# RWKV-7 features: no GpSimd products, the decay read one token over, both directions of a block together, the key norm in token layout; the q/k root of the DeltaNet projection moved up

## The reference, cut to what matters

```
w_log = -softplus(-(w0 + tanh(lw) @ w2)) - 0.5;  decay = exp(-exp(w_log))
a     = sigmoid(a0 + la @ a2);  gate = sigmoid(lg) @ g2
kk    = l2_normalize(heads(k * k_k))
k_dir = k * (1.0 + (a - 1.0) * k_a)
bonus = sum(r * k_dir[d] * u[d], channels of a head) * v, summed over d
```

## Time and profile before

| | |
|---|---|
| median of 3 runs | 4905.58 us (4900.68 to 4907.02) |
| the profiled execution | 4901.45 us, its span 4899.8 us |
| busy share of the span | PE 90%, PEld 80%, DVE 41%, ACT 28%, POOL 11% |
| mean granted TensorE clock | 0.939 |

### The profile page before, as it was taken

The page is one execution under the profiler, slowest core; times in us unless marked ns, Lnnn a source line. Parts: engine busy times, 40 slices in busy tenths (PEclk is TensorE's granted clock), DMA queues, the critical chain, the costliest instruction groups (busy, mean ns, idle before and its releaser), DMA issues. The chain is left out here.

```text
span 4899.8 us, 101076 instructions
## 1 busy us (share of the span) xinstructions
PE 4409.8 (90%) x43461; PEld 3932.3 (80%) x43461; DVE 1991.6 (41%) x2817; ACT 1366.0 (28%) x1958; POOL 532.2 (11%) x690
## 2 busy tenths in 40 slices
PE   6999989898948996999998999988998849996998
PEld 5998977887827995889897999977887629984887
DVE  3222254454475445322223222353444484446334
ACT  3211133232242222321113211243222242223322
POOL 1000000332032110000100000001321051100000
PEclk8999999999959998999999999999999859998999
DMA  5233231000200002233423222121000100012332
GB/s 199 79 111 109 71 112 39 14 1 4 60 7 3 4 4 78 78 124 95 154 77 112 66 62 60 59 62 35 1 0 24 47 1 4 4 42 75 97 94 69
DMA packets 344215, 286.50 MB, mean 58 GB/s; under 512 B 9086, under 2 KB 316772, under 8 KB 343396
## 3 DMA queue, kind: packets, MB, share of 16 engines
q1 hardware_dynamic: 326628, 218.92, 15.0%
q0 software_dynamic: 17280, 62.92, 3.7%
HBM read 270.27 MB, written 11.53 MB: 58 GB/s over the span
## 5 line engine op out<-in xcount | busy, mean ns | idle before, releaser
L646 PE MATMUL PS<-x_hi,w_hi 128*128 128x384 f32 (+1 forms) x2464 | 678.1, 344 | 17.6 <-DVE x_lo L550 16.1
L646 PE MATMUL PS<-x_lo,w_hi 128*128 128x384 f32 (+1 forms) x2464 | 676.3, 344 | 0.0
L646 PE MATMUL PS<-x_hi,w_lo 128*128 128x384 f32 (+1 forms) x2464 | 676.2, 343 | 0.0
L646 PEld LDWEIGHTS PS<-x_hi,w_hi 128*128 128x128 f32 x2464 | 450.3, 189 | 38.7 <-issue 24.4
L646 PEld LDWEIGHTS PS<-x_lo,w_hi 128*128 128x128 f32 x2464 | 450.2, 189 | 13.9
L646 PEld LDWEIGHTS PS<-x_hi,w_lo 128*128 128x128 f32 x2464 | 449.7, 189 | 13.7
L779 DVE TENSOR_TENSOR silu_buf<-silu_buf,PS 128x768 f32<-128x768 f32 (+1 forms) x88 | 78.1, 887 | 786.2 <-ACT silu_buf L712 786.2
L1896 PE MATMUL PS<-arena 64*64 64x64 f32 (+1 forms) x9216 | 356.9, 229 | 12.1 <-POOL arena L1879 5.6
L622 DVE TENSOR_TENSOR w_lo<-raw_w,w_hi 128x2048 fp32r<-128x2048 f32 x136 | 311.7, 2292 | 133.2 <-ACT w_hi L617 133.2
L690 PE MATMUL PS<-hidden_hi,w_hi 128*128 128x256 f32 (+1 forms) x1232 | 346.7, 351 | 19.3 <-DVE hidden_lo L784 19.3
L617 ACT ACTIVATE w_hi<-raw_w 128x2048 fp32r<-128x2048 f32 x136 | 259.5, 1908 | 338.5 <-PE PS L690 331.4
(11 more groups left out here) (341 smaller groups left out, 7803.5 us busy)
## 6 DMA issues: line engine op xcount, KB each, us to landing
raw_w<-in_ffn_w_dram SPq DMA_DIRECT2D x240, 512.0 KB, 4.4
arena<-in_ada_w_dram POOLq DMA_DIRECT2D x120, 512.0 KB, 6.1
arena<-in_w_in_dram SPq DMA_DIRECT2D x64, 512.0 KB, 3.9
arena<-in_ada_w_dram SPq DMA_DIRECT2D x6, 2048.0 KB, 14.6
raw_w<-in_ffn_w_dram SPq DMA_DIRECT2D x32, 384.0 KB, 3.5
arena<-in_w_out_dram SPq DMA_DIRECT2D x16, 512.0 KB, 4.2
h_save<-arena SPq DMA_DIRECT2D x16, 384.0 KB, 2.3
arena<-h_save SPq DMA_DIRECT2D x2, 3072.0 KB, 9.9
```

Of the source, the lines that this page charges most:

```text
L646: mm = pe.matmul(PS[:, 4 * b + 2 * g + s, 0:half], w[wo][:, k, g, :], x_split[xo][:, k, a + s * half:a + (s + 1) * half], start=(k == 0 an ...
```

## The change

- GpSimd has no work in the feature stage; its three products are made by DVE (`keys`).
- The decay up to the token before is no longer computed: KKP takes exp of minus `G` one token over within each chunk of 64 (pieces of 63), and the first token of a chunk is a copy of kk.
- The step from a to the key factor is ACT's Identity with scale and bias; the bonus is formed as (key0 u0 + key1 u1) r, the first product on ACT.
- A round is one block with both directions: gates of both, scans of both, exps of both in place of their arguments, products of both. ACT thus loads its tables once per round for Sigmoid and once for Exp.
- The first block's gates, scans and products come before the key norm. The norm's root is taken of 8 rows from one PSUM tile, turned into token layout (`pe_head_turn`), inverted as 48 columns, widened by ACT copies and spread by matmuls with the identity.
- In the DeltaNet projection the q/k root is taken at the end of place 10, between the Silus of places 9 and 10 (with a table load for each way), in place of after the last Silu.

The diff, cut to its core (of the features only the new lines; the old are printed above):

```diff
-        def pe_head_turn(pe):
+        def pe_head_turn(pe, rows=head_rows):
 
             for t in range(T // P):
-                mm = pe.transpose(PS[:, 6, 8 * t:8 * t + 8], head_rows[:, t * P:(t + 1) * P], ident[0:8, 0:8])
+                mm = pe.transpose(PS[:, 6, 8 * t:8 * t + 8], rows[:, t * P:(t + 1) * P], ident[0:8, 0:8])
...
-        HEAD_STEPS = 2 * NB + 2
+        HEAD_STEPS = 2 * NB + 3
...
                     finish(place - 1)
                     if place - 1 < 2 * NB:
                         square(place - 1)
+                if place == 2 * NB + 2:
+                    act.wait_ge(qk_summed, layer * HEAD_STEPS + 2 * NB)
+                    nc.scalar.activation(head_rows, RSTD[0:8, :], ACT.Sqrt, bias=eps[0:8, 0:1]).then_inc(qk_rooted, 1)
             finish(3 * NB - 1)
-            act.wait_ge(qk_summed, layer * HEAD_STEPS + 2 * NB)
-            nc.scalar.activation(head_rows, RSTD[0:8, :], ACT.Sqrt, bias=eps[0:8, 0:1]).then_inc(qk_rooted, 1)
 
             def split_place(place):
                 split(place // 2, place % 2)
 
             split_place(GATES + 2)
             act.wait_ge(proj_summed, 2 + layer * PT + GATES + 1)
+            act.wait_ge(conv_used, 2 + 3 * NB * (layer + 1))
...
-        E1, E2 = region(44544 + 3 * T, T), region(44544 + 4 * T, T)
+        fsq = region(46848, 2, T)
+        fsq_rows = fsq[0:8, 0, :]
+        KK_PLACE = [RSTD, PS[:, 4:6, :].rearrange("p b c -> p (b c)")[:, CTX:]]
+        KK_WIDE = [fsq[:, i, :].rearrange("p (t h c) -> p t h c", t=T // P, h=2) for i in range(2)]
+        K1 = lambda layer: 3 * NB * layer + NB
+        FE, FX = 16, 7
...
             sc = nc.scalar
             sc.activation(lora_w, lora_w, ACT.Tanh)
             sc.activation(lora_g, lora_g, ACT.Sigmoid).then_inc(lora_acted, 1)
...
             act.wait_ge(h_saved, 16 * KT * (layer + 1))
...
+            def gates(j, d):
+                J = NB * layer + j
+                act.wait_ge(lora_summed, 2 * J + d + 1)
+                if j > 0:
+                    act.wait_ge(fe_dve, FE * (J - 1) + (13 if d == 0 else 16))
                 for s, (a, w) in enumerate(SEGS):
...
+                    sc.activation(SG2[d][:, a:a + w], PS[:, 4 * d + s, 0:w], ACT.Sigmoid,
                                   bias=prm[:, layer, 1, B_W0 + d * NB + j:B_W0 + d * NB + j + 1])
...
+                    ins = sc.activation(AA2[d][:, a:a + w], PS[:, 4 * d + 2 + s, 0:w], ACT.Sigmoid,
                                         bias=prm[:, layer, 1, B_A0 + d * NB + j:B_A0 + d * NB + j + 1])
                 ins.then_inc(gates_ready, 1)
...
+                act.wait_ge(gates_ready, 2 * J + d + 1)
+                sc.activation(KD2[d], AA2[d], ACT.Identity, scale=prm[:, layer, 1, B_KA + j:B_KA + j + 1],
+                              bias=drv[:, 15 + j:16 + j]).then_inc(fe_exp, 1)
+            def decays(j, d):
+                J = NB * layer + j
+                act.wait_ge(fe_dve, FE * J + d + 1)
+                sc.activation(SG2[d], G2[d], ACT.Exp, scale=-DECAY_SCALE)
+                last = G2[d][:, RW_C - 1::RW_C] if d == 0 else G2[d][:, 0::RW_C]
                 pc = PC[:, d, j, :] if d == 0 else PC[:, d, j, ::-1]
                 sc.activation(pc, last, ACT.Exp, scale=-DECAY_SCALE).then_inc(fe_exp, 1)
...
+                act.wait_ge(fe_exp, FX * J + 3 + 2 * d)
+                sc.activation(G2[d], G2[d], ACT.Exp, scale=DECAY_SCALE).then_inc(fe_exp, 1)
+            for j in range(NB):
+                J = NB * layer + j
+                for d in range(2):
+                    gates(j, d)
+                if j == 0:
+                    for i in range(NB):
+                        act.wait_ge(kk_step, (1 + 2 * NB) * layer + i + 1)
+                        if i >= 2:
+                            act.wait_ge(kk_summed, K0(layer) + i - 1)
+                        sc.activation(fsq[:, i % 2, :], KK[:, i, :], ACT.Square).then_inc(kk_squared, 1)
+                for d in range(2):
+                    decays(j, d)
+                act.wait_ge(fe_dve, FE * J + 3)
+                sc.activation(BON[:, j, :], KD2[0], ACT.Copy, scale=prm[:, layer, 1, B_U + j:B_U + j + 1]).then_inc(fe_exp, 1)
+                if j == 0:
+                    act.wait_ge(kk_summed, K0(layer) + NB)
+                    sc.activation(fsq_rows, RSTD[0:8, :], ACT.Sqrt, bias=eps[0:8, 0:1]).then_inc(kk_rooted, 1)
+                    act.wait_ge(kk_step, (1 + 2 * NB) * layer + NB + 1)
+                    for i in range(NB):
+                        if i >= 2:
+                            act.wait_ge(kk_spread, K0(layer) + i - 1)
+                        sc.activation(KK_WIDE[i % 2], bc(tok_heads[:, :, 2 * i:2 * i + 2], 3, [P, T // P, 2, P // 2]),
+                                      ACT.Copy).then_inc(kk_squared, 1)
         def pe_feat(pe, layer):
...
             pe.wait_ge(lora_landed, 80 * (layer + 1))
             pe.wait_ge(lora_acted, layer + 1)
...
+            def lora(j, d):
+                if j > 0:
+                    pe.wait_ge(gates_ready, 2 * (NB * layer + j - 1) + d + 1)
                 rows = slice(64 * d, 64 * d + 64)
                 for o, (wt, src) in enumerate(((w2w, lora_w), (a2w, lora_a))):
                     for s, (a, w) in enumerate(SEGS):
...
+                        mm = pe.matmul(PS[:, 4 * d + 2 * o + s, 0:w], wt[rows, j * P:(j + 1) * P], src[rows, a:a + w],
                                        start=True, stop=True)
                 mm.then_inc(lora_summed, 1)
+            def spread(j):
+                pe.wait_ge(kk_squared, K1(layer) + NB + j + 1)
+                if j >= 2:
+                    pe.wait_ge(kk_step, (1 + 2 * NB) * layer + NB + j)
+                for t in range(T // P):
+                    mm = pe.matmul(KK_PLACE[j % 2][:, t * P:(t + 1) * P], fsq[:, j % 2, t * P:(t + 1) * P], ident[:, :],
+                                   start=True, stop=True)
+                mm.then_inc(kk_spread, 1)
+            lora(0, 0)
+            lora(0, 1)
+            pe.wait_ge(gates_ready, 2 * NB * layer + 2)
             for j in range(NB):
...
+                pe.wait_ge(kk_squared, K1(layer) + j + 1)
+                for a, w in SEGS:
+                    mm = pe.matmul(RSTD[0:8, a:a + w], to_pair_rows(j), fsq[:, j % 2, a:a + w], start=(j == 0), stop=(j == NB - 1))
+                mm.then_inc(kk_summed, 1)
+            lora(1, 0)
+            pe.wait_ge(kk_rooted, 2 * layer + 2)
+            pe_head_turn(pe, fsq_rows).then_inc(qk_summed, 1)
+            for j in range(NB):
+                spread(j)
+            pe.wait_ge(kk_step, (1 + 2 * NB) * (layer + 1))
+            lora(1, 1)
+            for j in range(2, NB):
+                for d in range(2):
+                    lora(j, d)
+            for j in range(NB):
+                pe.wait_ge(fe_dve, FE * (NB * layer + j + 1))
                 if j == 0:
                     pe.wait_ge(gates_ready, 2 * NB * (layer + 1))
                 for s, (a, w) in enumerate(SEGS):
...
         def dve_feat(dve, layer):
             v = nc.vector
...
+            mult = lambda out_, a, b: v.tensor_tensor(out_, a, b, ALU.mult)
             for j in range(NB):
                 v.tensor_scalar(KK[:, j, :], K_[:, j, :], prm[:, layer, 1, B_KK + j:B_KK + j + 1], None,
                                 ALU.mult).then_inc(kk_step, 1)
...
+            dve.wait_ge(h_saved, 16 * KT * (layer + 1))
+            def chunks(t):
+                return t.rearrange("p (c r) -> p c r", r=RW_C)
+            def scan(j, d):
+                way = (lambda t: t) if d == 0 else (lambda t: t[:, ::-1])
+                dve.wait_ge(gates_ready, 2 * (NB * layer + j) + d + 1)
+                v.tensor_tensor_scan(way(G2[d]), keep[:, :], way(SG2[d]), 0.0, ALU.mult, ALU.add).then_inc(fe_dve, 1)
+            def keys(j, d):
+                way = (lambda t: t) if d == 0 else (lambda t: t[:, ::-1])
+                J = NB * layer + j
+                at = FE * J + (10 if d == 0 else 13)
+                now, before = (slice(1, RW_C), slice(0, RW_C - 1)) if d == 0 else (slice(0, RW_C - 1), slice(1, RW_C))
+                mult(AA2[d], AA2[d], KK[:, j, :]).then_inc(fe_dve, 1)
+                dve.wait_ge(fe_dve, at + 1)
+                mult(way(BP[d][:, j, :]), AA2[d], G2[d]).then_inc(fe_dve, 1)
+                out_, kk = chunks(way(KKP[d][:, j, :])), chunks(KK[:, j, :])
+                first = slice(0, 1) if d == 0 else slice(RW_C - 1, RW_C)
+                v.tensor_copy(out_[:, :, first], kk[:, :, first])
+                mult(out_[:, :, now], kk[:, :, now], chunks(SG2[d])[:, :, before]).then_inc(fe_dve, 1)
             for j in range(NB):
...
+                J = NB * layer + j
+                way = lambda t: t[:, ::-1]
+                for d in range(2):
+                    scan(j, d)
+                for d in range(2):
+                    dve.wait_ge(fe_exp, FX * J + d + 1)
+                    mult(KD2[d], KD2[d], K_[:, j, :]).then_inc(fe_dve, 1)
+                for d in range(2):
```

(69 more changed lines are left out.)

62 lines of the change are left out of this document (3 added, 59 removed).

## The result

| | before | after |
|---|---|---|
| median of 4 runs, us | 4904.1 (4900.68 to 4907.02) | 4826.8 (4822.57 to 4829.57) |
| profiled execution, us | 4901.45 | 4829.57 (span 4828.0) |
| feature stage, each layer, us | 139.1 | 108.5 |
| DVE busy in that stage, us | 106.9 | 75.2 |

The kernel after takes 0.9842 of the time before [0.9825, 0.9859], 77.3 us less; 67 to 70 were forecast. By the two profiled executions it is 71.9 less: the one before lies 2.7 us under its median, the one after 2.8 above.

The account below looks back on a forecast made before the run. It took DVE, slowed by GpSimd, to bound the feature stage's units. 54.6 us from both feature stages plus 12.4 from the q/k root made 67 off 4901.45, 4834, stated as 4836 against the runs' median; range 4802 to 4864.

Parts of the forecast that it names:

- GpSimd's products make DVE's slow: Feature-stage units: a two-input DVE product over 128x768 takes 0.96 us with GpSimd at rest, 2.55 us beside it.
- Rival (f): Feature stage: 2.5 us is the products' own, not GpSimd's doing; 61 us slower, 4966 us, decided from 1.8 a product; chance 0.03.
- A round of 18.9 us: Feature stage, one block with both directions: 18.9 us (17.0 to 21) against 24.2, DVE waiting 0.5, 1.1 and 0.6.
- the floor of 17.0: Feature stage: DVE's own work in one block, both directions, if DVE never waits: 17.0 us.
- Rival (b): Feature stage and q/k root: DVE never waits and the clock is kept, 100 us less, 4803 us; chance 0.14.
- (c): Feature stage: ACT and DVE alternate, or Identity needs its own table; round 24 us, head 52, total 4878; chance 0.13.
- The lora products are hidden: Feature-stage rounds: the next round's lora matmuls, 5.5 us at the low clock, are covered by DVE's work.
- The head: Feature stage's start to t0 of the second block, key norm included: 48 us, between 40 (clock up) and 52.
- The stage's last terms: End of the feature stage: 2.9 us for the last keys and 4.2 us for the unchanged tail.
- The root: DeltaNet projection: q/k root moved one place up saves 6.2 us a layer, 12.4 in all; other ends 18.2 and 0.
- Rival (d): Projection: the root's move gains nothing, DVE's inverse or later places taking it back; 54.6 us saved alone, 4851; chance 0.04.
- rival (e): ACT in the later rounds: every table load costs its 1.28 us twice, 15 us more, 4851 us; chance 0.03.

## Why the prediction was right

It was right, with the time 0.2% under the forecast and in the range. By its own steps:

- **GpSimd's products make DVE's slow.** Shown, from both sides: 0.95 us each once GpSimd's products are gone from the kernel before, 2.04 in the mean once idle ones are put into the kernel after. Rival (f), which needed 1.8 a product, falls.
- **A round of 18.9 us.** 18.83, with each of its three waits within 0.13. The walk came nearer than the floor of 17.0 that was given with it: without its waits the round is 16.3. The estimates in it: Identity 1.03 (1.0 taken), KKP 0.94 (0.9 taken, bound 2.5), the 12-element copy 0.17 (0.1 taken). Rival (b), DVE without a wait, would need those 16.3; (c), a round of 24, is out. The run with one direction after the other has what (c) priced, more handovers, and even there the round is 21.66.
- **The lora products are hidden.** 6.86 us in that round beside DVE's work, and no engine waited for them in rounds 1 to 3.
- **The head.** 45.2 us against 48: a mis-sized term. (The forecast's own terms behind the root, with the spreads at 10.6, add up to 48.8.) Two pieces were shorter. The forecast charged 5.5 us for each of two lora units, one after the other, up to 15.5; but the 7.19 us of the earlier trace rows are both units, and here both took 7.38 and ended at 12.0. So ACT was free for the squares at 16.1, ahead of the 16.5 to 18.6 forecast, and its root ended at 30.7 and not at 32. And the spreads took 8.2 us, between the 6 and the 10.6 of the two clock levels, at a granted clock of 0.69.
- **The stage's last terms.** 45.2 + 3 x 18.83 = 101.7 leaves 6.8 us for the 2.9 and 4.2, 7.1.
- **The root.** The wait at L847 is gone, and the stop of 4.5 is 4.25. The low clock held for 6.8 us (some 7 forecast), but 1.8 of them lay inside the stop, so that 5.0 us of work ran at half speed, an estimated 2.5 us lost for the 2.9. The projection became 8.0 and 8.2 us shorter for the 6.2 forecast, of which up to 1.4 is how long the clock was low behind the old stop in that one execution. Rival (d) falls with the run of the move alone, 11.2 us less. In the run that took the stop away the clock stayed up and 6.1 and 5.6 more were gained.
- **Table loads cost 1.28 once,** rival (e) falls: the load at 1420.85 starts 0.02 us behind the end of the Identity ahead of it, and the next ACTIVATE starts at 1422.14; a drain would also have shown up in a round of 18.83 that was walked without it. The Trainium skill (ScalarE: Activation LUTs, What ACT_TABLE_LOAD costs) has a drain there of about the load's own length; these rounds don't show it.
- **What was not in the sum:** the stages that nobody touched, 5.6 us longer here, 5.0 of it the two DeltaNet scans. Why was not tried; the stretches of low clock in them differ (near the start of the first scan one of 3.4 us before is one of 6.8 after, by an estimate 1.7 us of the 2.5).
- **Some luck in the number.** By the profiled executions the feature stages saved 6.6 us more than forecast (61.2 for 54.6, 5.6 of it in the two heads) and the root 3.8 more (16.2 for 12.4), and the untouched stages gave 5.6 back: 71.8 for 67. The misses partly cancel. The forecast's last step also slipped by 2 us: 4834 and 4.1 are 4838, not 4836.

## What to carry to other kernels

Before giving GpSimd a share of elementwise work, read the mean of DVE's two-input products beside it and alone: here DVE made 24 products more in a layer and ended 11 us sooner. Walk one round with both engines' queues: 2.5 of the 18.8 us of a round were waits that neither engine's busy time shows, and they grew to 5.3 when a result crossed from DVE to ACT and back twice as often, with table loads inside. Where a stop of TensorE ends with a small instruction of another engine, look what stands ahead of that one in its queue: half a microsecond of reciprocal, moved ahead of a convolution, gave about 6 us a layer. Read a gain from the length of its stage, from start to start, and not from when the next stage starts: here the two differ by 1.4 us.

## What the runs showed of the hardware

- Beside GpSimd's products, DVE's scan was slowed too (2.98 us for 1.76), and even a copy of 12 elements with one input, 1.44 us for 0.17; beside fills one such copy took 0.57. The two-input product in 12 pieces of 63 was the exception, 0.93 beside GpSimd, as alone. Why is open; it was not tried with other pieces.
- GpSimd's own product took 2.20 us beside a busy DVE, its fill of the same size 0.74.
- The reciprocal's time went with its length per partition and not with its elements: 8 x 768 took 4.94 us, 128 x 48, as many elements, 0.46. Other shapes were not tried.
- With the stop of 4.25 us TensorE was granted 0.50 for 6.8 us in either layer, from 1.8 us before the stop's end; without the stop the same spread took 1.50 us in place of 2.93. The low stretch behind a stop is not of one length: behind that of 10.83 us it was 6.6 us in one kernel, and 3.7 behind the same stop in another.
